# Projection weight loads placed one slot further ahead in the sync engine's written order

## The reference

```python
hn = rms_norm(x, norm_mix)
proj = einsum('bsd,dn->bsn', hn, w_in) + b_in
qkv = proj[..., OFF_QKV:OFF_Z_ATT].reshape(b, s, 3, 3, 4, 128)  # group, q/k/v, head, channel
q, k = rope(rms_norm(q)), rope(rms_norm(k))
for g, (window, dilation) in enumerate(((128, 1), (512, 4), (2048, 16))):
    o_g, lse_g = dilated_window_attention(q[:, :, g], k[:, :, g], v[:, :, g], window, dilation)
```

## Time and profile before

| | before |
|---|---|
| median of three runs | 1331.48 us |
| time of the profiled execution | 1330.25 us |
| its span, first to last instruction | 1328.4 us |
| PE matmul busy | 1312.6 us, 99% of the span |
| DVE, ACT, POOL busy | 55%, 36%, 39% |
| share of PE in the chain that ended last | 91% |
| mean granted TensorE clock | 0.998 of full speed |

### The profile page before, as it was taken

One profiled execution on the slowest core, in us unless ns is written; L12 is line 12 of the kernel. 1 busy time (PEld: TensorE's weight loads), 2 busy tenths in 40 slices (PEclk: granted clock), 3 DMA queues, 4 the chain that ended last, 5 costly groups with the idle time before them and its releaser, 6 DMA issues.

```text
span 1328.4 us, 17821 instructions
## 1 busy us (share of the span) xinstructions
PE 1312.6 (99%) x6070; PEld 1088.4 (82%) x6070; DVE 736.1 (55%) x1352; ACT 476.5 (36%) x1186; POOL 516.8 (39%) x500
## 2 busy tenths in 40 slices
PE   9999999999999799999999999999999999999998
PEld 6887888888888688888888888888888888888887
DVE  6799888852656365665666551257412457134323
ACT  7455656642324243343442677221100011223100
POOL 7976424404275542222322424341175316045020
PEclk9999999999999999999999999999999999999999
DMA  6232322332354344544535456376279534022111
GB/s 249 77 107 80 98 77 80 108 104 75 69 129 101 83 108 108 135 102 105 133 90 131 119 150 181 110 246 229 79 293 407 190 123 166 40 80 64 40 40 48
DMA packets 215386, 164.72 MB, mean 124 GB/s; under 512 B 116448, under 2 KB 172032, under 8 KB 215296
## 3 DMA queue, kind: packets, MB, share of 16 engines
q1 hardware_dynamic: 175008, 87.76, 24.4%
q10 hardware_dynamic: 40288, 75.82, 16.1%
HBM read 121.42 MB, written 42.09 MB: 123 GB/s over the span
## 4 chain that ended last, share of the span: by engine, by line
PE 91%; DVE 4%; POOL 2%; ACT 1%; DMA 1%; issue 0%; SPq 0%; POOLq 0%; ACTq 0%
PE bank L1318 28%; PE bank L1323 28%; PE bank L1322 28%; PE bank L1466 2%; PE bank L1446 2%; POOL hn L615 1%; PE bank L1455 1%; DVE xc L1048 1%; PE bank L1559 1%; PE bank L1363 0%; DMA gain_mix<-in_gain_mix 0%; POOL ring L595 0%; DVE ibuf L1075 0%; DVE tbuf L1067 0%; DVE y_lo L1084 0%
## 5 line engine op out<-in xcount | busy, mean ns | idle before, releaser
L599 POOL TENSOR_SCALAR ring<-raw 128x512 fp32r<-128x512 f32 x221 | 161.4, 730 | 726.7 <-PE bank L1323 516.1
L595 POOL TENSOR_TENSOR ring<-raw,ring 128x512 fp32r<-128x512 f32 x221 | 315.3, 1427 | 18.4
L1318 PE MATMUL bank<-hn,ring 128*128 128x512 f32 x640 | 252.0, 394 | 1.6 <-DVE sgbuf L1036 1.2
L1323 PE MATMUL bank<-hn,ring 128*128 128x512 f32 x640 | 249.4, 390 | 0.0
L1322 PE MATMUL bank<-hn,ring 128*128 128x512 f32 x640 | 249.0, 389 | 0.0
L1318 PE MATMUL bank<-ring,hn 128*128 128x512 f32 x576 | 233.6, 406 | 6.8 <-POOL hn L615 6.8
L1323 PE MATMUL bank<-ring,hn 128*128 128x512 f32 x576 | 226.0, 392 | 0.0
L1322 PE MATMUL bank<-ring,hn 128*128 128x512 f32 x576 | 225.6, 392 | 0.0
L1318 PEld LDWEIGHTS bank<-hn,ring 128*128 128x128 f32 x640 | 120.2, 188 | 26.9 <-DVE sgbuf L1036 1.6
L1323 PEld LDWEIGHTS bank<-hn,ring 128*128 128x128 f32 x640 | 120.1, 188 | 25.5
L1322 PEld LDWEIGHTS bank<-hn,ring 128*128 128x128 f32 x640 | 120.3, 188 | 24.0
(11 more groups left out here) (180 smaller groups left out, 2057.8 us busy)
## 6 DMA issues: line engine op xcount, KB each, us to landing
raw<-in_w_tail_s SPq DMA_DIRECT2D x104, 256.0 KB, 3.1
turn_dram<-qkr SPq DMA_DIRECT2D x384, 32.0 KB, 1.8
qkT<-turn_dram SPq DMA_DIRECT2D x96, 128.0 KB, 2.1
g_in<-gate_dram ACTq DMA_DIRECT2D x48, 256.0 KB, 3.6
raw<-in_w_rnn_s SPq DMA_DIRECT2D x45, 256.0 KB, 2.6
raw<-in_w_qkv_s SPq DMA_DIRECT2D x48, 192.0 KB, 2.8
gate_dram<-g_out ACTq DMA_DIRECT2D x32, 256.0 KB, 2.2
raw<-in_w_qkv_s SPq DMA_DIRECT2D x48, 128.0 KB, 2.7
```

Source lines behind the costliest of these rows:

```text
L595: nc.gpsimd.tensor_tensor(ring[:, ring_slot(p), 1], raw[:, p % RAW], ring[:, ring_slot(p), 0].bitcast(F32), ALU.subtract).then_inc(w_ready, 1)
L599: nc.gpsimd.tensor_scalar(ring[:, ring_slot(p), 0], raw[:, p % RAW], 1.0, 1.0, ALU.mult, ALU.mult).then_inc(hi_cut, 1)
L1318: ins = T.matmul(out, lhs[0], rhs[0], start=first, stop=False)
L1323: return T.matmul(out, lhs[1], rhs[0], start=False, stop=last)
```

## The change

`loaded_after` looks one slot further ahead for the projection slots. Nothing else is edited.

```diff
 def loaded_after(G):
 
     if G < SLOTS_Q:
-        c, s = divmod(G, NT)
+        c, s = divmod(G + 1, NT)
         return FIRST_QKV + KD * (c + 1) + (KD // 2 if s < 2 else KD)
     return FIRST_TAIL + max(KD, G - SLOTS_Q + 11)
```

## The result

| | before | after |
|---|---|---|
| median | 1331.6 us (4 runs, 1330.89 to 1332.26) | 1320.78 us (4 runs, 1320.64 to 1320.81) |
| ratio | | 0.9921, 95% interval 0.9909 to 0.9933 |
| profiled execution: time, span | 1330.25, 1328.4 us | 1320.64, 1318.6 us |
| PE waits for the copy | 6.8 us | none |

The kernel is 0.8% faster: 10.8 us by the medians, 9.8 us by the two profiled spans. The prediction had 1321.6 us, and 1318.54 us of span.

A forecast was written before the change was run, and what follows sets the result against it. PE's matmuls were taken to bound the kernel, with only the wait for POOL's copy to win: 1331.48 less 9.86 us, all other terms 0, gives 1321.6 us; range 1320.5 to 1323.7.

The forecast's parts named there:

- What bounds, and which wait goes: PE's matmuls are busy for 99% of the span; its largest wait, 6.8 us for POOL's copy of hn, goes.
- The price of the wait: PE's steps 22 to 24 against the equal steps 14 to 16: 20.08 less 10.22, so 9.86 us.
- Step 1: On SP, chunk 4's first-half load moves ahead of tiles 17 and 18, issued at about 409.77, 10.14 us earlier.
- Step 2: On POOL, first cut 3.53 us behind the load's issue, at 413.3; the copy starts at 421.15 and ends at 439.99.
- slow case: Longest of the other times from a load's issue to its first cut, 4.22 us, leaving PE 1.2 us to spare.
- rival A: Chunk 4's load lands late beside ACT's bias load, so part of the wait stays: 1322.0 or 1323.1 us; chance 0.08.
- Step 3: PE's slot 28: block 7 begins at 441.8 and needs the copy's end at 439.99, 1.8 us to spare.
- Steps 4 and 5: SP's tiles pushed back, tile 17's stores by 2.2 us, likewise at seven other boundaries and second halves: charged 0.
- rival D: SP falls behind at chunk boundaries; from 12 us of lateness PE waits for qkT in L1446: 1334.4 us; chance 0.04.
- The sum: Span 1328.40 - 9.86 = 1318.54 us; the same amount off the median, 1331.48 - 9.86 = 1321.6 us.
- Rival B: PE's clock did not fall in the timed runs, so only 8.4 us are won: 1323.1 us; chance 0.08.
- Rival C: The copy does not come earlier because something else holds POOL, so the time stays at 1331.5 us; chance 0.06.

The follow-up runs named there:

- Two slots ahead: The changed kernel's projection loads placed two slots ahead in place of one; measured 1320.69 us (1320.56 to 1320.89).
- three slots ahead: The changed kernel's projection loads placed three slots ahead in place of one; measured 1357.51 us, ratio 1.0213.
- the four experiments at full speed: Kernel before with only chunk 4's load moved, 1320.56 us, or only the copy, 1320.89; changed kernel with bias load moved, 1320.63, or loads two slots ahead, 1320.69.
- half-way kernel: Kernel before with the load of pieces (4,0) to (4,3) placed between tiles 17 and 18; measured median 1324.46 us of five runs.

## Why the prediction was right, point by point

**What bounds, and which wait goes.** Right, and shown by runs that part the two: the moved load of chunk 4 alone gives all, the others nothing, and the copy moved without any load gives the same.

**The price of the wait, 9.86 us.** Right: measured 9.86 between steps 22 and 24. Taking it from two stretches with the same matmuls was the step that mattered; the 6.8 us that the list of waits shows would have been 3 us short.

**Step 1, the issue at 409.77.** Measured 409.82.

**Step 2, the end of the copy at 439.99.** Measured 441.02. The first cut came 0.9 us later than worked out, 4.39 us behind the issue, where I had 3.53 and 4.22 as the slow case. That is rival A's mechanism, ACT's bias load next to SP's, in a small size: with that load moved away it is 2.90 us. By its bound of 3.3 us the lateness would have reached PE; the measured 1.5 us did not. The Trainium skill ("DMA: Bandwidth & Descriptors", "Issuing engines are not separate DMA queues") has both engines' DMAs on the same 16 DMA engines, and the first-half loads of this pair of profiles agree. The 3.53 us that the sum took from the old place were no floor: other loads came down to 2.7 us, and up to 4.6.

**Step 3, block 7 at 441.8, with 1.8 us to spare.** It began at 441.88; 0.86 us were to spare. Enough, but half of what was worked out: a bias load that had cost 2.4 us in place of 1.5 would have shown. That none of the gain was lost is in part luck.

**Steps 4 and 5, no charge for SP's lateness.** The charge of nothing was right, but the lateness of tile 17 was mis-sized and one user of a tile was left out. Its stores went out at 414.27 (worked out: 413.6), but took SP 3.04 us and not 1.81 to issue, and the fetch came at 419.47 in place of 414.47: 5.0 us later, where I had 2.2. PE used the tile at 428.59, 7 us behind a usual landing. The least cover of any tile after the change is 5.7 us (fetch at 542.74, use at 550.49), more than the 4.3 of tile 64 before.

I took PE's 12 us as the cover of a tile and made it rival D's turning point. The tile has a second user with less cover, 7 us: DVE, which wants the buffer of the tile two before. But DVE's cover is not the turning point either. Two slots ahead DVE waits up to 3.6 us and nothing is lost, since what stands behind DVE has slack of its own; three slots ahead it waits up to 7.4 us and the kernel loses 36 us, where my own expectation from PE's cover was at most 11. The turning point lies between the two. Of my argument against D ("7.8 us is the worst pile-up that I can put together") the size was not contradicted: after the change the latest fetch comes 9.5 us behind DVE's write (426.58 to 436.09), 6.5 us more than the usual 3.0.

**The sum.** 1318.54 us of span, measured 1318.6. On the median it was 0.8 us off: 1321.6 for 1320.78, well inside the range. The step that was off is "the profiled execution is 1.23 us below the median, and the same amount comes off". That amount was not a constant. It goes with the mean clock, which differs from run to run (next point), and it went with the wait. After the change the profiled execution is only 0.14 us below the median.

**Rival B, the clock.** The mechanism is real, in both directions. Of 22 runs of the kernel before beside the experiments, two show a mean clock of 1.000, and they take 1328.61 and 1329.26 us, 7.8 and 8.5 us above the changed kernel's 1320.78 (I had 8.4 for the wait alone). The others show 0.996 to 0.998 and take 1330.2 to 1332.0. So the clock adds 1 to 3 us in nearly every run, the profiled one (1330.25) being among the lightest; that is why the medians differ by 10.8 us and not by 9.86.

**Rival C** did not come about.

## What to carry to other kernels

Where engines follow one written order, look at what stands behind a load in the stream of the engine that takes it in: here nobody waited for the weights, but a copy was queued behind their cut. Price a string of short waits by the distance between two landmarks against an equal stretch elsewhere, since the list of waits leaves out slow issue and the clock. When a step is pushed back, work out the cover of each of its users, the producer that wants its buffer back too; the consumer's need not be the smallest. Then follow the stall through what is written behind it: an overrun cover costs nothing until the slack behind it is used up (3.6 us of DVE's waiting were free here, 7.4 were not).

## What the runs showed of the hardware

A wait of some 8 us in PE's stream made the run time itself uneven. The kernel before spreads over 3.7 us (1328.61 to 1332.26 us in all runs), and its mean granted clock goes with it (1.000 at the low end, 0.996 at the high end); without the wait all runs of the changed kernel and of the four experiments at full speed lie between 1320.42 and 1321.17 us, at 0.999 to 1.000. In the half-way kernel the same program ran at 1324.3 or 1326.4 us, with a mean clock of 0.999 to 1.000 or of 0.998; the one of these runs that has a trace, at 1326.19 us, shows the fall behind the copy. In the traces a fall inside the wait cost nothing that could be seen, one behind it 1.5 to 1.9 us. Whether the fall comes in a given run could not be told from anything in the traces, and stays open.
